# Two transformer blocks on one core: half-size products in both blocks, their weight sums on GpSimd

## The reference

```python
def first_block(...):
    h = rmsnorm(x, attn_norm_w[l])
    z = h @ w_in[l]
    hq, hf, hi, hg, cq, ckv, kr, gate_a, gate_b = jnp.split(z, split_idx, axis=-1)
    o_a = hgrn2_mixer(hq, hf, hi, hg, lb_all[l], hg_out_norm_w[l]).astype(x.dtype)
    o_b = mla_mixer(cq, ckv, kr, positions, ...)
    y = jax.nn.sigmoid(gate_a) * (o_a @ w_branch_hgrn[l]) + jax.nn.sigmoid(gate_b) * (o_b @ w_branch_mla[l])
    x = x + y @ w_out[l]
    x = x + hierarchical_moe(rmsnorm(x, ffn_norm_w[l]), ...)      # 64 experts, top 2 of one group
    return rmsnorm(x, final_norm_w)

def hybrid_layer(x, mem, ...):                                    # the second block
    z = rmsnorm_2(x, g_in) @ w_in
    (mq, mk, mv, mg, dq, dk, dv, dg, iq, ik, iw, xq, xg, glog) = jnp.split(z, offs, axis=-1)
    ya, yb, yc = moba(mq, mk, mv), dsa(dq, dk, dv, iq, ik, iw), cross(xq, mem)
    gates = jax.nn.sigmoid(glog + b_merge)
    u = gates[0] * (ya*silu(mg) @ w_up_moba) + gates[1] * (yb*silu(dg) @ w_up_dsa) + gates[2] * (yc*silu(xg) @ w_up_cross)
    return x + u @ w_out
```

## Time and profile before

| | us |
|---|---|
| median of 3 runs | 1601.19 (1600.17 to 1602.2) |
| the profiled execution's own time | 1599.81 |
| its span, first to last instruction | 1598.0 |
| PE matmul busy | 1270.6 (80%) |
| DVE busy | 450.5 (28%) |
| ACT busy | 198.6 (12%) |
| POOL busy | 0.5 |
| HBM read | 504.91 MB, 317 GB/s over the span |

### The profile page before, as it was taken

The page is one execution under the profiler, slowest core; times in us unless marked ns, Lnnn a source line. Parts: engine busy times, 40 slices in busy tenths (PEclk is TensorE's granted clock), DMA queues, the critical chain, the costliest instruction groups (busy, mean ns, idle before and its releaser), DMA issues.

```text
span 1598.0 us, 19255 instructions
## 1 busy us (share of the span) xinstructions
PE 1270.6 (80%) x8526; PEld 776.0 (49%) x8526; DVE 450.5 (28%) x788; ACT 198.6 (12%) x402; POOL 0.5 (0%) x5
## 2 busy tenths in 40 slices
PE   9999999999746856656656665565676999989998
PEld 8656887864313412212212221221221578989985
DVE  3254343232100100100101010010010477698522
ACT  2002023120000000000000000000000211135411
POOL 0000000000000000000000000000000000000000
PEclk9999999999988877877877877887788999999999
DMA  9342256389999999999999999999999654424340
GB/s 387 110 181 107 87 182 256 161 359 402 442 427 437 431 433 430 437 435 433 438 431 436 430 436 431 438 428 440 431 436 426 262 200 159 159 106 164 114 158 27
DMA packets 20558, 506.90 MB, mean 317 GB/s; under 512 B 4240, under 2 KB 4368, under 8 KB 6544
## 3 DMA queue, kind: packets, MB, share of 16 engines
q1 hardware_dynamic: 20208, 505.70, 75.6%
q10 hardware_dynamic: 288, 0.26, 0.0%
HBM read 504.91 MB, written 1.05 MB: 317 GB/s over the span
## 4 chain that ended last, share of the span: by engine, by line
PE 56%; DMA 39%; DVE 3%; issue 1%; ACT 0%; SPq 0%; DVEq 0%; ACTq 0%
DMA ring<-in_experts 37%; PE psP L1218 23%; PE psP L655 9%; PE psP L1270 6%; PE psP L703 4%; PE psP L1268 4%; DMA arena<-in_experts 2%; PE psA L718 2%; PE psP L1371 1%; PE psB L1588 1%; DVE arena L1869 1%; PE psB L1204 1%; PE psA L634 1%; DVE ring L1869 0%; PE psP L1317 0%
## 5 line engine op out<-in xcount | busy, mean ns | idle before, releaser
L655 PE MATMUL psP<-arena 128*32 128x512 f32 x1024 | 145.3, 718 | 130.8 <-DMA arena<-in_experts 130.6
L655 PE MATMUL psP<-ring,arena 128*32 128x512 f32 x1024 | 146.0, 721 | 129.8 <-DMA ring<-in_experts 129.8
L1869 DVE TENSOR_TENSOR X<-X,psA 128x512 f32<-128x512 f32 x66 | 45.3, 688 | 695.5 <-PE psA L718 681.4
L1218 PE MATMUL psP<-arena,ring 128*128 128x256 f32 x896 | 196.1, 379 | 0.0
L1218 PEld LDWEIGHTS psP<-arena,ring 128*128 128x128 f32 x896 | 169.2, 190 | 23.0 <-issue 0.3
L655 PEld LDWEIGHTS psP<-ring,arena 128*32 128x32 f32 x1024 | 37.2, 129 | 235.2 <-issue 231.5
L655 PEld LDWEIGHTS psP<-arena 128*32 128x32 f32 x1024 | 35.1, 129 | 235.4 <-DMA arena<-in_experts 120.2
L1218 PE MATMUL psP<-ring,arena 128*128 128x512 f32 (+2 forms) x368 | 141.9, 543 | 0.0
L1218 PEld LDWEIGHTS psP<-ring,arena 128*128 128x128 f32 x368 | 65.9, 190 | 67.5 <-issue 67.0
L703 PE MATMUL psP<-arena 128*32 128x512 f32 x512 | 66.8, 681 | 26.9 <-DMA arena<-in_experts 25.6
L703 PE MATMUL psP<-ring,arena 128*32 128x512 f32 x512 | 65.9, 667 | 25.8 <-DMA ring<-in_experts 24.5
(11 more groups left out here) (339 smaller groups left out, 1161.9 us busy)
## 6 DMA issues: line engine op xcount, KB each, us to landing
arena<-in_experts SPq DMA_DIRECT2D x7, 4096.0 KB, 21.3
ring<-in_experts SPq DMA_DIRECT2D x7, 4096.0 KB, 22.7
ring<-in_u_gl SPq DMA_DIRECT2D x6, 2048.0 KB, 8.2
ring<-in_u_hq SPq DMA_DIRECT2D x2, 2048.0 KB, 23.5
ring<-in_u_hv SPq DMA_DIRECT2D x2, 2048.0 KB, 12.1
ring<-in_u_hg SPq DMA_DIRECT2D x2, 2048.0 KB, 9.2
ring<-in_u_ga SPq DMA_DIRECT2D x2, 2048.0 KB, 8.6
ring<-in_u_gb SPq DMA_DIRECT2D x2, 2048.0 KB, 8.9
```

Source lines behind the costliest of these rows:

```text
L655: mm = pe.matmul(z[j * CAP:(j + 1) * CAP, :], x[:, 4 * half + k, j * CAP:(j + 1) * CAP], held[c % 4][:, k // 2, j, (k % 2) * 512:(k % 2 + ...
L1218: mm = pe.matmul(dsts[o], lhs_of(o, k), rhs_of(o, k), start=(k == 0), stop=(k == kc - 1))
L1869: return dve.tensor_tensor(o, a, b, op)
```

## The change

Fifteen units of the first block (hq0, hq1, hv0, hv1, cl, hg0, hg1, ga0, ga1, gb0, gb1, wa0, wa1, wb0, wb1) and dq of the second are computed in seven products as well. All four sums of weights of the first block's units are made by GpSimd. In the second block GpSimd makes the first two for every unit, and all four for dq and for xg and gl0 to gl5, which are the units beside the softmax turns; VectorE keeps t2 and t4 of the other eight. "halves" is done four times, for each of the activations h, oa, ob and the second h. For the new units t4 is written over weights in the slot, after product 1 has read them. `merge` keeps two temporaries instead of four, so ScalarE's copy waits (`spent`) until the previous unit is put together. The results of wa and wb now pass through SBUF before they are multiplied with their gates. The first load of experts waits until wa1 has been gated instead of until TensorE has finished it.

```diff
+FIRST = ["hq0", "hq1", "hv0", "hv1", "cl", "hg0", "hg1", "ga0", "ga1", "gb0", "gb1", "wa0", "wa1", "wb0", "wb1"]
+FAST = FIRST + ["dq", "dv", "dk", "mv", "mq", "dg", "mk", "mg", "xq", "xg", "gl0", "gl1", "gl2", "gl3", "gl4", "gl5"]
+HALVES = ["x", "oa", "ob", "mid"]
+ALL_BY_POOL = {"dq", "xg", "gl0", "gl1", "gl2", "gl3", "gl4", "gl5"}
...
-    proj("hf0", "hf1", "hq0", "hq1", "hv0")
+    proj("hf0", "hf1")
+    p.append(("halves", "x", ""))
+    proj("hq0", "hq1", "hv0")
...
-            p.append(("head", ("ga0", 20), ""))
+            p.append(("head", ("ga0", 40), ""))
             p.append(("cnorm", 0, "AB"))
         proj(fill[n - 1])
         if fill[n - 1] == "ch":
-            p.append(("head", ("hg0", 2), ""))
+            p.append(("head", ("hg0", 4), ""))
...
     proj("wa1")
+    p.append(("halves", "ob", ""))
+    p.append(("gated", "wa1", ""))
     p.append(("mnorm", 0, ""))
     proj("wb0", "wb1")
...
-    turn(6, 7, "xg", then=[("topk", 1)], after="gl0")
+    turn(6, 7, "xg", then=[("topk", 1)])
...
-                    wait_full(sp, ("proj", {0: "wa1", 2: "wb1", 3: "wo1"}[c]))
+                if c < 2:
+                    wait_empty(sp, ("proj", ("wa1", "wb1")[c]))
+                else:
+                    wait_full(sp, ("proj", {2: "wb1", 3: "wo1"}[c]))
...
         @block.gpsimd
         def _(pool):
+            def first_two(arg):
+                w, t1 = unit_ap(arg), sums_of(arg)[0]
+                wait_unit(pool, arg)
+                difference(t1, w[:, 0:4, high], w[:, 0:4, low])
+                pool.wait_ge(pool_summed, POOL_T1[arg])
+                difference(w[:, 0:4, high], w[:, 4:KC, high], w[:, 0:4, high])
+            def fourth_in_place(arg):
+                pool.wait_ge(made, 2 * FAST.index(arg) + 1)
+                fourth(arg)
...
+            for group in (FIRST[:11], FIRST[11:]):
+                for q, arg in enumerate(group):
...
+                    if arg in last_used:
+                        wait_full(pool, ("proj", last_used[arg]))
+                    first_two(arg)
+                    if q:
+                        fourth_in_place(group[q - 1])
...
+                    third(arg)
+                fourth_in_place(group[-1])
...
+            for q, arg in enumerate(FAST[len(FIRST):]):
+                if q >= 2:
+                    wait_full(pool, ("proj", FAST[len(FIRST) + q - 2]))
+                first_two(arg)
+                if arg in ALL_BY_POOL:
+                    third(arg)
+                    fourth(arg)
...
-            def add_up(arg, part):
+            def add_up(arg):
                 w, (t1, t2, t4) = unit_ap(arg), sums_of(arg)
+                dve.wait_ge(pool_summed, POOL_T1[arg] + 1)
+                tt(t2, w[:, 4:KC, high], t1, ALU.subtract).then_inc(summed, 1)
+                dve.wait_ge(summed, SUMMED[arg])
+                tt(t4, w[:, 4:KC, low], t2, ALU.subtract).then_inc(summed, 1)
...
-                p1, u2, w5, w7 = (as_quarter(arg, x) for x in kept_at)
+                p1, u2 = w5, w7 = [as_quarter(arg, x) for x in kept_for(arg)]
```

More of the change, by code:

```diff
@@ L185, in sums, with turn @@
     def sums(name):
-        p.extend([("sums", (name, 0), ""), ("sums", (name, 1), "")])
-    def turn(g, following, *names, then=(), after=None):
+        p.append(("sums", name, ""))
+    def turn(g, following, *names, then=()):
         if following is not None:
             soft(following)
-        if after:
-            p.append(("sums", (after, 0), ""))
         if g == 0:
-            p.append(("head", ("wa0", 3), ""))
+            p.append(("head", ("wa0", 6), ""))
         p.append(("probsT", g, "B"))
@@ L232, in plan @@
     p.append(("hg_outT", 0, "AB"))
+    p.append(("halves", "oa", ""))
     proj("kn0", "kn1")
@@ L273, in plan @@
     proj("iq", "ikw")
-    p.append(("head", ("dq", 4), ""))
+    p.append(("head", ("dq", 8), ""))
     p.append(("ropeT", "iq", "AB"))
     p.append(("ropeT", "ik", "AB"))
-    p.append(("halves", "h", ""))
+    p.append(("halves", "mid", ""))
     sums("dv")
@@ L305, in plan @@
     p.append(("normal", 6, ""))
-    sums("xg")
     proj("xq")
-    turn(6, 7, "xg", then=[("topk", 1)], after="gl0")
[L309 to L313, removed]
+    turn(6, 7, "xg", then=[("topk", 1)])
+    turn(7, 8, "gl0", then=[("topk", 2)])
+    turn(8, 3, "gl1", then=[("topk", 3)])
+    turn(3, 4, "gl2")
+    turn(4, 5, "gl3")
+    turn(5, 9, "gl4")
     turn(9, 10, "gl5")
@@ L1191, in _, with difference, third, fourth @@
         def _(pool):
+            low, high = slice(0, 256), slice(256, 512)
+            def difference(out, a, b):
+                pool.tensor_tensor(out, a, b, ALU.subtract).then_inc(pool_summed, 1)
+            def first_two(arg):
[4 more added lines that the diff above has]
+                difference(w[:, 0:4, high], w[:, 4:KC, high], w[:, 0:4, high])
+            def third(arg):
+                w, (t1, t2, _) = unit_ap(arg), sums_of(arg)
+                difference(t2, as_sums(w[:, 4:KC, high], t2), as_sums(t1, t2))
+            def fourth(arg):
+                w, (_, t2, t4) = unit_ap(arg), sums_of(arg)
+                pool.wait_ge(pool_summed, POOL_T2[arg])
+                difference(as_sums(t4, t2), as_sums(w[:, 4:KC, low], t2), t2)
+            def fourth_in_place(arg):
+                pool.wait_ge(made, 2 * FAST.index(arg) + 1)
+                fourth(arg)
+            last_used = {"hv0": "hq0", "hv1": "hq1", "cl": "hv0", "hg0": "hv1", "hg1": "cl", "ga0": "hg0", "ga1": "hg1",
+                         "gb1": "ga1", "wb0": "wa0", "wb1": "wa1"}
+            for group in (FIRST[:11], FIRST[11:]):
+                for q, arg in enumerate(group):
+                    if arg == "hq1":
+                        wait_full(pool, ("proj", "hf0"))
+                        wait_empty(pool, ("root_row", "x"))
+                    if arg in ("wa0", "wa1"):
+                        wait_full(pool, ("hg_out", 0))
+                    if arg in last_used:
+                        wait_full(pool, ("proj", last_used[arg]))
+                    first_two(arg)
+                    if q:
+                        fourth_in_place(group[q - 1])
+                    if arg == "gb0":
+                        wait_full(pool, ("cnorm", 0))
+                    third(arg)
+                fourth_in_place(group[-1])
             pool.wait_ge(rounds_ready, 1)
```

176 lines of the change are left out of this document (116 added, 60 removed).

## The result

The changed kernel takes 1605.22 us, median of 20 runs (1601.49 to 1609.24); the kernel before, run beside it, 1600.63 (1599.37 to 1602.2). The ratio is 1.0029, 95% interval 1.0022 to 1.0036: slower by 0.29%, where 1578 was forecast. The profiled execution of the changed kernel is its longest, 1609.24 us with a span of 1607.4, so what its trace shows adds up to some 5 us more than the medians differ by (9.4 us between the spans, 4.6 between the medians). Its runs spread over 7.7 us, those of the kernel before over 2.8; experiment 2 has what may be a reason.

What follows compares the result with a forecast made beforehand. TensorE was taken to bound both blocks, DMA the experts' stage between, VectorE one stretch. 1599.8 - 23.4 - 5.4 + 1.0 + 5 = 1577.0, plus 1.4 to the median: 1578 us; 8-of-10 range 1568 to 1592.

Steps and rivals of the forecast that it cites:

- TensorE's units: First block and dq: ten units by features and six by tokens in seven products save TensorE 23.4 us.
- the 1.0 at wa1: After wa1, VectorE's late additions and halves stall TensorE before product 6 of wb0: 1.0 us charged.
- the 1.7 forecast: Second block: dq in seven products instead of plain gains 1.7 us.
- The turns: Second block, softmax turns: without VectorE's sums, TensorE's waits of 4.1 and 1.3 us go, gaining 5.4 us.
- The price of a sum: One GpSimd weight sum taken as two passes over 128 x 1024, 2.5 us, between 1.2 and 3.7.
- the case in which it sets the pace: Rival, first block: GpSimd's sums take 4.4 us and limit each unit; 1644 us, chance 0.08.
- The stream of the experts: Experts' stage: its loads hang on TensorE's progress, so it moves with the first block and the gain passes through.
- The waits between VectorE and GpSimd: The two engines holding each other up at levels, cnorm and after wa1: 5 us taken, bounds 0 and 16.
- The high end: Upper bound of VectorE-GpSimd waits, 16 us: levels 5, cnorm overrun by 6, halves after wa1 5.
- full exclusion: Rival: VectorE's multiplications and GpSimd's sums never overlap, mostly alternate; cost 16 instead of 5, 1589 us, chance 0.26.
- The reserves: First block, VectorE's slack before TensorE needs results: level 3 0.3 us, cnorm 0.5; after wa1 a stall.
- the main case: Whole kernel: VectorE-GpSimd waits cost 5 us, about a third of the high end; 1578 us, chance 0.52.

Runs made afterwards that it cites:

- experiment 2: Changed kernel with GpSimd's first two sums held back, gb0's until the cnorm transposes and wb1's until the halves of ob are made: 1594.85 us.
- The run with the turns alone: Kernel before, with only the sums of xg and gl0 to gl5 moved, all four each, from VectorE to GpSimd: 1592.26 us.
- experiment 1: Changed kernel with each GpSimd weight sum cut to 8 of 256 columns, TensorE multiplying by loaded weights instead; output not the reference's: 1571.45 us.
- experiment 7: Changed kernel with dq made plainly again, so GpSimd has no sums before dv's: 1598.41 us.
- Experiment 5: Kernel with sums cut to 8 columns, plus VectorE repeating the first of the halves of ob 12 times: 1582.18 us.

## Why the prediction was wrong

**TensorE's units, 23.4 us: right but for about a tenth.** With the collisions taken away the landmark stands 19.6 us before the old one, where the ten units by features and the five by tokens of the first block were to bring 21.7 less the 1.0 at wa1. And dq: from iq to dv 33.4 us with it in seven products, 34.6 plain, 1.2 for the 1.7 forecast. (The slices were misread, without effect: TensorE is at 9 in the first ten, not eight.)

**The turns, 5.4 us: right in place, small in size.** The run with the turns alone gave 7.5. The missing 1.7 us are in the profile of before, the 32 matmuls after the wait at 5.44 us against 3.74 elsewhere.

**The price of a sum, 2.5 us: near, in part by luck**, 2.35 us where VectorE is not in the way. It was set at two passes since that lay between two bounds, and the runs do not bear the passes out: a copy, which reads and writes once, takes 1.04 us and a fill 0.95, some four tenths of a sum. In the changed kernel no wait of a microsecond was for GpSimd; the case in which it sets the pace did not come.

**The stream of the experts: right.** The first block ends 5.6 us later and so does that stage: the first product of iq went from 1261.55 to 1267.11. In experiment 1 the landmark comes 19.6 us earlier than before, and iq 19.0.

**The waits between VectorE and GpSimd, 5 us with bounds of 0 and 16: this step failed.** Experiment 1 against the changed kernel puts them, with the slow stretches that follow them, at 33.8 us (1605.22 - 1571.45), twice the bound. The spans of the two traces differ by 37.2; what follows divides those. In the first block 25.3 us at the landmark, 24.5 of which reach iq: 2.0 at the levels, 8.4 at cnorm, 7.8 at wb0, 1.1 at the transposes of the attention's inputs, and 4.8 of slow matmuls behind cnorm (1.33 and 1.27 for 0.77 and 0.71, 3.62 for 1.95) and in wb0 (5.85 for 3.84 of 32); 24.1 of the 25.3. From iq to dv 10.2, behind dv 2.5. Three things were missed:
1. The high end counted 5 us at the levels, 6 at cnorm and 5 behind wa1. At the levels 2.0 came; at cnorm 8.4, since four sums stood there in a row and the last one held up the first scaling as well (0.42 to 2.29 us), an instruction without a second tensor to read, which the count had left out; behind wa1 7.8, since four sums and not two met the gating and the halves (11.31 us for 3.76). Short instructions get as long a wait as long ones.
2. The head of the second block was costed at a gain of 1.7 for dq. It lost 8.7 us there in the profiled execution (34.8 to 43.6; experiment 7 has 6.8 by the medians), on operations of 128x2 that nobody would count as work. The question "what does VectorE do while these four sums run, and who waits for it" was asked in the first block and not here.
3. A stall of TensorE was priced at its length. Experiment 5 has 2.0 us on top of 8.7, and the slow matmuls at cnorm and in wb0 are 4.8 of the 25.3.

The rival called full exclusion had the mechanism and gave it 16 us and 0.26; with the right size it would have been a kernel slower than before. The reserves were found in the right places (cnorm with 0.5 us, halves of ob with none), and I then let the main case take a third of the price, on the argument that a single sum in the way was likelier than all of them; at both places four in a row stood there. Two small slips in the sums change nothing: without waits they give 1572.0 and not 1571.8, and 14.8 against 13.5 is 1.3 and not 1.2.

## What to carry to other kernels

Work moved to an idle GpSimd was free here beside VectorE instructions that read PSUM, and not beside those on SBUF alone. Lay the two engines' timelines over each other, and count each VectorE instruction on SBUF that TensorE waits for as up to one whole GpSimd instruction longer, however small it is. Where such a chain stands, hold GpSimd back with a wait until it is through, if nobody wants its sums before (with three edits of the order and one unit given up, this was worth 24 us); where no gap is left, as at dq, leave the work as it was.

## What the runs showed of the hardware

- Both engines pay: a sum of 2.35 us takes 3.3 in alternation, a multiplication of 1.21 us as part of a pair of 3.3.
- A VectorE operation on 128x2, 0.18 us, took 2.1 us on the mean of two beside sums of 128x1024. Copies of 1.04 us in place of sums of 2.35 brought the loss of four multiplications from 4.5 to 1.6 us.
- A GpSimd instruction that only writes leaves a two-input multiplication alone (4.87 us for four) and slows a scaling from 0.42 to 1.09 us.
- After a wait of 8.9 us TensorE's next 192 matmuls took 2.0 us more; after one of 4.1 us, 1.7 on 32; after 8.4 us the granted clock of the window from 150 to 160 was 0.50.
- Two traces with the same second block differ by 5.1 us between iq and dv (43.6 and 38.5), with a VectorE operation 0.05 us behind the start of a sum in one and 0.28 us ahead of it in the other.
